# Queries and keys prepared inside the q/k/v projection, and one channel tile of the convolution by ScalarE products and accumulating DMAs

## The reference

```python
proj = h @ w_in[l]                                   # q | k | v | glu_in
k_ctx = rms_norm(kv_ctx[..., :KV_COLS]..., k_norm_w[l])
q = apply_axial_rope(rms_norm(q, q_norm_w[l]), cos, sin)
k = apply_axial_rope(rms_norm(k, k_norm_w[l]), cos, sin)
attn_out = windowed_gqa_with_context(q, k, v, k_ctx, v_ctx, sink)   # window +-128, softmax with sink
ga, gb = jnp.split(glu_in, 2, axis=-1)
u = ga * jax.nn.sigmoid(gb)
u = depthwise_conv(u, conv_w[l], conv_b[l])          # 31 taps over positions
u = jax.nn.silu(layer_norm(u, conv_norm_w[l], conv_norm_b[l]))
mix = jnp.concatenate([attn_out, u], axis=-1) @ w_out[l]
x = x + g1 * mix
# then: rms_norm, modulate, w_up, width-3 convolution, silu(gate) * val, w_down, gate g2
```

## Time and profile before

| | us |
|---|---|
| median of 3 runs | 1344.73 (1341.78 to 1345.15) |
| profiled execution | 1338.05 |
| its span | 1336.2 |
| TensorE busy | 1227.3 (92%) |
| VectorE busy | 706.0 (53%) |
| ScalarE busy | 429.0 (32%) |
| GpSimd busy | 171.4 (13%) |

### The profile page before, as it was taken

How to read it: one execution, slowest core, us unless ns; L and a number is a source line. 1 busy time by engine, 2 the same in 40 slices (tenths; PEclk the granted TensorE clock), 3 DMA queues, 4 the chain that set the end, 5 groups by cost and what they waited for, 6 DMA issues and landing times. The chain is left out here.

```text
span 1336.2 us, 15995 instructions
## 1 busy us (share of the span) xinstructions
PE 1227.3 (92%) x6181; PEld 1014.5 (76%) x6181; DVE 706.0 (53%) x950; ACT 429.0 (32%) x831; POOL 171.4 (13%) x146
## 2 busy tenths in 40 slices
PE   6899998259999989989999999999999969999997
PEld 1378887148998967878888888888888858887886
DVE  1489999866566553344434343434344344447445
ACT  4542144355665673443222222222222111111110
POOL 2100000359929100000000000000000000004001
PEclk9899999559999989999999999999999989999999
DMA  9222100015512123213111111111111041113112
GB/s 382 67 76 76 55 1 1 1 64 158 160 62 80 48 90 132 79 48 95 48 48 47 47 47 47 47 47 48 52 55 49 1 157 47 47 48 110 47 47 79
DMA packets 77988, 94.79 MB, mean 71 GB/s; under 512 B 5866, under 2 KB 59234, under 8 KB 76916
## 3 DMA queue, kind: packets, MB, share of 16 engines
q1 hardware_dynamic: 75796, 87.65, 20.2%
q10 hardware_dynamic: 1152, 4.19, 0.8%
q0 software_dynamic: 992, 2.29, 0.5%
HBM read 85.74 MB, written 8.39 MB: 70 GB/s over the span
## 5 line engine op out<-in xcount | busy, mean ns | idle before, releaser
L1281 PE MATMUL ps<-hx,uph 128*128 128x512 f32 x672 | 261.4, 389 | 0.0
L1282 PE MATMUL ps<-hx,uph 128*128 128x512 f32 x672 | 261.4, 389 | 0.0
L1285 PE MATMUL ps<-hx,upl 128*128 128x512 f32 x672 | 206.8, 389 | 0.0
L1083 DVE TENSOR_TENSOR upl<-up_raw,uph 128x1024 fp32r<-128x1024 f32 x44 | 53.8, 1226 | 263.9 <-ACT uph L1080 263.9
L1080 ACT ACTIVATE uph<-up_raw 128x1024 fp32r<-128x1024 f32 x44 | 46.6, 1060 | 339.4 <-PE ps L1285 328.5
L1414 PE MATMUL ps<-dnh,ah 128*128 128x512 f32 x352 | 138.0, 392 | 13.2 <-DVE al L1465 13.2
L1285 PEld LDWEIGHTS ps<-hx,upl 128*128 128x128 f32 x672 | 126.1, 188 | 26.2
L1282 PEld LDWEIGHTS ps<-hx,uph 128*128 128x128 f32 x672 | 126.2, 188 | 26.1
L1281 PEld LDWEIGHTS ps<-hx,uph 128*128 128x128 f32 x672 | 126.1, 188 | 26.2
L1415 PE MATMUL ps<-dnl,ah 128*128 128x512 f32 x352 | 137.5, 391 | 0.0
L1416 PE MATMUL ps<-dnh,al 128*128 128x512 f32 x352 | 137.4, 390 | 0.0
(11 more groups left out here) (241 smaller groups left out, 2169.8 us busy)
## 6 DMA issues: line engine op xcount, KB each, us to landing
up_raw<-in_w_up SPq DMA_DIRECT2D x44, 512.0 KB, 3.8
wm<-in_w_mod SPq DMA_DIRECT2D x32, 512.0 KB, 3.8
dn_raw<-in_w_down SPq DMA_DIRECT2D x44, 256.0 KB, 2.6
wm<-in_w_mod SPq DMA_DIRECT2D x8, 1024.0 KB, 20.2
xs<-in_x ACTq DMA_DIRECT2D x8, 512.0 KB, 14.5
gw_raw<-in_w_in SPq DMA_DIRECT2D x8, 512.0 KB, 4.0
wo_raw<-in_w_out SPq DMA_DIRECT2D x8, 512.0 KB, 3.4
xt<-in_x SPq DMA_DIRECT2D x8, 512.0 KB, 5.2
```

Source lines behind the costliest of these rows:

```text
L1083: dve.tensor_tensor(out=upl[:, g], in0=up_raw[:, g], in1=f(uph[:, g]), op=ALU.subtract).then_inc(up_lo, 1)
L1281: pe.matmul(o, uph[:, g, k, :], hx[:, k, 0, c_], start=(k == 0), stop=False)
L1282: pe.matmul(o, uph[:, g, k, :], hx[:, k, 1, c_], start=False, stop=False)
L1285: last = pe.matmul(o, upl[:, g, k, :], hx[:, k, 0, c_], start=False, stop=(k == KT - 1))
```

## The change

Five things are done together.

Block 2 is gone. Its work stands in block 1 beside the projection of q, k and v: each token tile is rotated straight out of PSUM by VectorE (`rotated`), with unscaled values; the keys get their reciprocal root afterwards, the queries not at all: the exponential's scale and the maximum's factor take it per row (`msq`). The squares are summed by one ScalarE square and one VectorE reduction. Three sets of four transposes each of a finished tile (one for k, two for q: `items`; a context tile has one) stand among the matmuls of the tile after the next, after k steps 2, 4 and 6. The projection has three pairs of banks in turn (`slot`), the transposes have the other two banks. Latent keys and queries are written back into the columns of `hx` that the projection has already read.

The convolution's channel tile 1 (`AT`) is no longer VectorE's. ScalarE multiplies the whole row by tap i (31 products of 1024 elements, `product`), the first two of them straight into two accumulators; GpSimd issues a DMA for each later one that adds it to one of the accumulators (`add_product`), in turn. VectorE adds the two in group 8. A product waits for the transfer of the product two before.

The other tiles have 3 x 51 taps: 86 of them beside the gated unit, two in each latent tile of the projection, the rest six a group in the attention (two with each of the first two maxima, one with each of the others). The layer norm is therefore in groups 9 to 12, its reciprocals in 13 and 14.

The four modulation sections run side by side; GpSimd multiplies a loaded tile as before, and an accumulating DMA adds it to the section's sum. GpSimd issues one product's DMA (24 to 30) ahead of the four sections' DMAs of each k.

The output's low halves are stored under other tile numbers (`out_rows`), and the loads of `w_out` wait for group 8.

```diff
+        TAP_QKV = (0, 0) + (2,) * TT
+        TAP_GRP = 6
+        DVE_TILES = (0, 2, 3)
+        AT = 1
+        SUM = [cacc[:, AT, :], conv_y[:]]
+        P_BLOCK = 24
+        def product(act):
+            i = prods[0]
+            prods[0] += 1
+            dst = SUM[i] if i < 2 else ring(i)
...
+            elif i >= 4:
+                act.wait_ge(sum_in[i % 2], 16 * (i // 2 - 1))
+            act.activation(dst.rearrange("p (two s) -> p two s", two=2), by_parity(u_plain[:, i:i + T]), ACT.Identity,
...
+        def add_product(pool, i):
+            pool.wait_ge(prod_done, i + 1)
+            if i >= 4:
+                pool.wait_ge(sum_in[i % 2], 16 * (i // 2 - 1))
+            pool.dma_start(SUM[i % 2], ring(i), accum_op=ALU.add).then_inc(sum_in[i % 2], 16)
...
+            def slot(m):
+                return 2 * (m % 3)
...
+                def turn(it):
+                    m, kind = items[it]
...
+                    if it >= 2:
+                        pe.wait_ge(qkT_out, it - 1)
+                    if kind == "k":
+                        pe.wait_ge(k_lo, m + 1)
...
+                        if m >= 2 and k in (2, 4, 6) and turned < items_upto[m - 1]:
+                            turn(turned)
+                            turned += 1
...
                 for m in range(NK):                                     # ScalarE
+                    while m >= 2 and placed < items_upto[m - 1]:
+                        place(placed)
+                        placed += 1
...
+                    act.activation(sqb[:, h0:, :], ps[...], ACT.Square).then_inc(sqb_done, 1)
+                    act.activation(vraw[:, m], ps[...], ACT.Copy).then_inc(v_out, 1)
+                    product(act)
+                    act.wait_ge(ssq_done, m + 1)
+                    act.activation(msq[:, m, h0:], msq[:, m, h0:], ACT.Sqrt, bias=eps_c).then_inc(root_done, 1)
+                    act.wait_ge(k_rot, m + 1)
...
                 for m in range(NK):                                     # VectorE
...
+                        rotated(flat(kk), flat(kr), ps[:, b + 1, 0:NG * HD], 0, t, NG, None, k_mul)
...
+                        rotated(qa[:, m % 2, :], qb[:, m % 2, :], ps[:, b, :], 2, t, NH, None, q_mul)
+                    dve.wait_ge(sqb_done, m + 1)
+                    dve.reduce_sum(msq[:, m, h0:], sqb[:, h0:, :], axis=AX.X).then_inc(ssq_done, 1)
...
+                    taps(dve, TAP_QKV[m])
+                    dve.wait_ge(k_hi, 2 * (m + 1))
...
             def _(pool):                                                # attention
-                for n in range(NMOD):
...
-                    pool.tensor_tensor(out=dst[:], in0=dst[:], in1=w, op=ALU.add).then_inc(mod_acc, 1)
+                for k in range(KT):
+                    if P_BLOCK + k < TAPS:
+                        add_product(pool, P_BLOCK + k)
+                    for a in range(NW):
+                        pool.wait_ge(wm2_in[a], 16 * (k + 1))
+                        pool.tensor_scalar(wm2[:, a, :], wm2[:, a, :], nat[:, k, 0:1], 1.0, ALU.mult, ALU.mult).then_inc(mod_mul, 1)
...
+                        pool.dma_start(sums[a][:], wm2[:, a, :], accum_op=ALU.add).then_inc(mod_acc[a], 16)
...
+                    elif n == LN - 1:                                   # VectorE, group 8
+                        for r in range(2):
+                            dve.wait_ge(sum_in[r], 16 * len(range(2 + r, TAPS, 2)))
+                        dve.tensor_tensor(out=cacc[:, AT, :], in0=cacc[:, AT, :], in1=conv_y[:], op=ALU.add).then_inc(tap_done, 1)
...
+                        if j == 2 and P_BLOCK + n < TAPS:               # ScalarE, groups 0 to 6
+                            product(act)
```

More of the change, by code:

```diff
@@ L255, in _ @@
                 pool.memset(u[:], 0.0).then_inc(pad_done, 1)
+                for i in range(2, P_BLOCK):
+                    add_product(pool, i)
             @block.tensor
@@ L448, in _ @@
+                while placed < len(items):
+                    place(placed)
+                    placed += 1
             @block.vector
@@ L737, in build @@
         NW = 4
-        wm2 = at(18, "wm2", [P, NW, D])
+        wm2 = at(51, "wm2", [P, NW, D])
+        sums = [at(kib, f"sums{a}", [P, D]) for a, kib in enumerate((67, 71, 75, 120))]
         pbuf = [at(129, "p0", [P, GQ, SW]), at(83, "p1", [P, GQ, SW])]
@@ L787, in _ @@
             def _(pool):
[L788 to L789 removed]
+                for a in range(NW):
+                    pool.memset(sums[a][:], 0.0).then_inc(zero_done, 1)
                 muls = 0
[L791 to L808 removed]
@@ L810, in head_steps @@
+                pool.wait_ge(rec5, 4)
+                for ct in range(CTL):
+                    pool.tensor_tensor(out=cacc[:, ct, :], in0=cacc[:, ct, :], in1=rstd[:], op=ALU.mult).then_inc(scaled, 1)
             def head_steps(n):
@@ L906, in _ @@
                     values(n, m - 1)
-                for c, dst in enumerate((shift2, scale2)):
-                    pe.wait_ge(mod_acc, (2 + c) * KT)
+                for c in range(2):
+                    pe.wait_ge(mod_acc[1 + c], 16 * KT)
                     pe.wait_ge(pt_out, first_item[NGRP])
                     for j in range(KT):
-                        last = pe.matmul(ps[:, 4, c * KT + j:c * KT + j + 1], dst[:, j * P:(j + 1) * P], ones[:, 0:1], start=True, stop=True)
+                        last = pe.matmul(ps[:, 4, c * KT + j:c * KT + j + 1], sums[1 + c][:, j * P:(j + 1) * P], ones[:, 0:1], start=True, stop=True)
                 last.then_inc(col_mm, 1)
-                pe.wait_ge(mod_acc, NMOD)
                 for r in range(2):
+                    pe.wait_ge(mod_acc[3 * r], 16 * KT)
                     for hh in range(2):
-                        pe.matmul(ps[:, 2 * r + hh, :], ones[:], (g1b, g2b)[r][:, half(hh)], start=True, stop=True).then_inc(row_mm, 1)
+                        pe.matmul(ps[:, 2 * r + hh, :], ones[:], sums[3 * r][:, half(hh)], start=True, stop=True).then_inc(row_mm, 1)
                 turn_outputs(NGRP - 1)
@@ L1028, in _ @@
                             maxima(n + 1, j)
+                            if n < LN:
+                                taps(dve, TAP_GRP if n == LN - 1 and j == 3 else TAP_GRP // 4 + (j < TAP_GRP % 4))
                         if j == 2:
```

571 lines of the change are left out of this document (278 added, 293 removed).

## The result

| | before | after |
|---|---|---|
| median, same chip (4 runs each) | 1344.94 us | 1359.72 us |
| ratio, 95% interval | | 1.0105 (1.0074 to 1.0136) |
| profiled execution, its span | 1338.05, 1336.2 us | 1354.87, 1353.0 us |
| first score matmul | 289.61 us | 257.90 us |
| first score to the end of the last group | 187.7 us | 234.5 us |

A forecast was written before the change was run, and what follows sets the result against it. VectorE's preparation of queries and keys was taken to bound 61.2 us, TensorE being nearly full in projection and attention. -32.0 + 24.5 gave -7 or -8, from the median 1344.73 to 1338 us; 8 in 10 from 1309 to 1366.

The forecast's parts named there:

- Step 1: Before the attention: preparation stage goes, projection grows; first score matmul at 257.6 instead of 289.6, gain 32.0 us.
- The rival of the projection's chain: In the projection: ScalarE's second product or a late copy pushes each tile to 11.5 us; +10, 1348 us; chance 0.10.
- Step 3: In the attention: adding transfers fill the DMA engines, a step 17.7 us, VectorE waits 21.5 in group 8; loss 24.5.
- step 2: In the attention without transfers: taps +4, GpSimd's sums gone -6.6, scalings and reciprocals +4; rounded up, +1 us.
- no queue: In the attention: adding transfers hold the engines like copies, a step about 11.5 us; -31, 1314 us; chance 0.25.
- Transfers decide, slower than before: In the attention: adding transfers hold the engines 3.3 us, a step 23.1, wait 52; +23, 1368 us; chance 0.23.

The follow-up runs named there:

- the mended kernel: Against the kernel with 1328.7: the sink's addition stands behind the first maximum, its exponential ahead of the third copy; 1318.31 us, 0.9821.
- the kernel of the two order edits: Against the kernel with products issued at every second sum: ScalarE's product at the group's end, VectorE's taps 1, 1, 1, 3; 1332.27 us, 0.9909.
- the kernel with 1328.7: Against the kernel of the two order edits: the accumulators' sum and four reciprocals moved behind the last maximum of their group; 1328.73 us, 0.9892.
- the kernel with copies: Against the changed kernel: the 32 transfers of the modulation sums copy instead of adding, products still add; 1343.34 us, 0.9992.

## Why the prediction was wrong

The time from the first score, by groups, us to the product that ends each (profiled executions; the last three columns are kernels of the experiments, each with the edits of the one before and more):

| groups | before | after | products earlier | and order, reciprocals | and sink's addition |
|---|---|---|---|---|---|
| 0 | 21.4 | 16.9 | 16.8 | 16.8 | 16.9 |
| 1 to 7 | 84.5 | 95.2 | 90.7 | 81.5 | 76.8 |
| 8 to 12 | 58.0 | 85.8 | 73.1 | 70.3 | 69.8 |
| 13 to 15 | 23.5 | 36.3 | 37.7 | 38.0 | 33.5 |

**Step 1, the preparation stage: right.** First score at 257.90 for 257.6, gain 31.7 for 32.0, the wait in the third tile 5.8 for 5.7. The rival of the projection's chain is refuted: the tiles stand 9.4 to 9.6 us apart, not 11.5, and the chain had 3 us to spare, not 0.3.

**Step 3, the transfers: right in mechanism, price and place.** An adding transfer holds the engines 2.73 us for 2.53, a step is 17.3 for 17.7, the wait is in group 8. The forecast's 24.5 us behind the first score hold the +1 of step 2, so 23.5 were for the transfers; they cost 13 to 16 (the changed kernel against the one with products issued earlier), because VectorE itself came late, at 376 instead of 355: the groups before had grown. That the last transfer lands 12 us behind its issue, not 6, was missed; and the groups behind the wait were to take 10.7 to 14 us, where four of them took 14.2 to 17.1.

**Step 2, the attention without its transfers, "+1": this failed.** It measured +31.1 in the kernel where no transfer binds, and that turned -7 into +15. The sentence that failed is "six taps a group on VectorE beside 5.1, 9.1 of 10.66, never early for the next score: I charge 0.5 a group". Its terms, +4, -6.6 and +4, add up to +1.4 before anything is rounded, so the "+1" left nothing for the seven products on ScalarE. I had filled VectorE by its busy sum and not followed the chain. Laid against the mended kernel (the last column), whose attention takes 197.4 us behind the first score (255.15 to 452.5), the 31.1 divide like this:
- groups 1 to 7, 14 us, charged at under 4: 9 go with taps ahead of the maxima and the product ahead of two copies, 5 more with the sink's addition, nearly all in group 2. One execution tells this only roughly: the kernel of the two order edits, the same up to group 8, took 86.4 for 81.5;
- groups 8 to 12, 3 us. They go with the order of taps and products (70.2 in the kernel that has no more than that), so the sum's place in front of a maximum has no share that shows;
- groups 13 to 15, 4 us. Not the reciprocals' place: moved behind the last maximum they stood ahead of the sink's addition instead, and the three groups took 38.0 for 37.7. The 4.5 came off when the addition moved too;
- what the mended kernel still has over the one before, 9.7. Its groups 0 to 7 are 12 shorter than before and groups 8 to 12, where the layer norm now stands, 12 longer; groups 13 to 15 are 10 longer (33.5 against 23.5), where reciprocals, the root and GpSimd's scalings were charged at 4 in all.

The wait in group 15 costs once more behind the attention: the modulation's sums over partitions took TensorE 8.9 us before (476.7 to 485.6); in the mended kernel they start at half clock and take 12.8 (451.8 to 464.6).

Inside these sits a thing that the forecast left out. It credited 6.6 us for GpSimd's two-input sums gone, and with taps on VectorE they are indeed better gone (21 us and more when put back); but the multiplications that stayed hold VectorE too. In the kernel with products issued earlier one tap of 46 was long (1.66 us), and the sink's addition in eight groups (0.8 to 1.75 us for 0.15). Leaving the multiplications out took 7 us off the kernel with 1328.7 (ratios 0.9892 and 0.9841, their intervals just overlap); with the sink's addition moved they may stay.

The exponentials and maxima of the changed kernel have one per-row operand more: an exponential of 640 columns takes 0.88 us for 0.80, a maximum's factor 0.27 for 0.21. No run takes that back alone; the mended kernel's groups of 10.8 us, against 10.66, leave it little.

The rivals: "no queue" is refuted by the price of a transfer and the wait. The 3.2 us that the forecast estimated there for one transfer, by the fit in the Trainium skill's "DMA: Bandwidth & Descriptors", section "Anatomy of one DMA — SWDGE (gpsimd) path", don't hold for one that adds: it landed after 4.5 us in the projection and after 8.6 with the engines full. "Transfers decide, slower than before", came nearest in its sign but not in its cause: its step of 23.1 and its wait of 52 did not occur. Slower came from a step that no rival questioned. That the range, 1309 to 1366, held the time was luck: it was made wide for transfers, and the error was elsewhere. Not tried: how much of the last three groups' 10 us another place for reciprocals, root and scalings would give back.

## What to carry to other kernels

Work put beside a loop that is full to nine tenths is not priced by the busy sum of its engine but by what stands directly behind it on the chain: put it behind the last instruction that the critical engine waits for, on every engine at once, because either edit alone brought nothing here and both together 12 us. Where a transfer that somebody waits for shares a queue with transfers that nobody waits for, count its turn in the issuing engine's order; issuing it earlier gave 13 to 16 us with no work saved. Before moving work out of one instruction's way, see whose way it then stands in: the reciprocals moved from a maximum to the sink's addition. A small instruction ahead of the first copy of a loop pass is a lever: moved behind the first maximum, with its exponential ahead of the third copy, it was worth 10 us (ratios 0.9892 and 0.9821), half in group 2 and half in the last three groups.

## What the runs showed of the hardware

- A GpSimd multiplication with one input tile held VectorE's instructions that read two tiles from SBUF: 1.76 us for 0.15, up to 2.4 us for a tap of 0.74. Without the multiplications no tap was over 0.75. Its additions with two inputs held them more often: 35 of 46 taps over 1.2 us, groups of 17 to 18 us.
- A gap of 2.2 us on TensorE was followed by some 9 us at a granted clock of 0.50, with TensorE busy throughout, and cost the group 5 us; gaps of 0.88 and 0.52 close together also ended at 0.50. A gap of 1.48 us by itself (group 1 with the taps alone moved) left it at 1.00.
- An adding transfer of 512 KB within SBUF holds the 16 DMA engines 2.73 us, a copy 1.3; it lands 8.6 us after issue with the engines full and 4.5 in the projection (median of 22, at a share of 0.49 to 0.57).
- GpSimd's issue took 0.85 to 0.88 us for an adding transfer, where a plain one took 0.56, and 0.57 within SBUF in the kernel with copies. The products' took 1.17 to 1.18 from 302 on in the changed kernel, but 0.84 to 0.85 where they are issued earlier; why, no run shows.
